# Turning the inner rows of a feed-forward block on VectorE and through DRAM instead of on TensorE

## The chip, the cores and the metric

The kernel runs on one core of a Trainium2 chip. The metric is the device time of one execution, in microseconds (us). Engines: TensorE (PE), VectorE (DVE), ScalarE (ACT), GpSimd (POOL) and SyncE (SP, which here only issues DMA transfers).

## The reference

Two transformer blocks on 256 rows of width 1024, all float32. They hold four feed-forward parts, f0 to f3, which the change touches; the mixers between them stay as they are.

```
def swiglu(h, w_gu, w_down):
    g, u = jnp.split(h @ w_gu, 2, axis=-1)      # 1024 -> 2 x 2816
    return (jax.nn.silu(g) * u) @ w_down        # 2816 -> 1024

x = x + 0.5 * swiglu(rmsnorm(x, ffn1_norm), ffn1_wgu, ffn1_wdown)        # f0
...                                                                      # mixer
x = x + 0.5 * swiglu(rmsnorm(x, ffn2_norm), ffn2_wgu, ffn2_wdown)        # f1
x = x + gate * e
x = x + 0.5 * gt1 * rmsnorm_2(swiglu_2(h, w_gu1, w_dn1), g_post)         # f2
...                                                                      # mixer
x = x + 0.5 * gt3 * rmsnorm_2(swiglu_2(h, w_gu2, w_dn2), g_post)         # f3
mods = silu(c) @ w_ada + b_ada     # 1024 -> 9 x 1024, gives sc, sh, gt
```

## The kernel before, in words

**Products.** Each float32 operand is split into a high and a low half (`hi` rounded to fp32r, `lo` the rest), and a product is three matmuls: hi x hi, hi x lo, lo x hi. The weights come through a ring: SP loads "units" of 512 KB into `raw` (8 places; `load_unit` waits until PE has used the unit seven places back, `used`), ACT makes `w_hi` (L636, `hi_part`), DVE makes `w_lo` (L1151, `lo_part`), and PE takes 12 matmuls of 512 columns for a unit. ACT and DVE run through the same order of units; `w.to(n)` in their programs handles all units up to n + 1. A unit of the up product is two transfers of 256 KB (L522, L523), with runs of 1 KB.

**A feed-forward part.** `ffn_part(f)` stands once in each engine's program. `up` is the first unit of the up product, `dn` that of the down product. The inner width 2816 is handled in 11 blocks j (`UPB`) of 256 columns, four units each. PE accumulates gate and up columns of block j in PSUM (`acc(t, j % 2)`, t = 0, 1 the row tiles of 128); ACT takes SiLU of the gate columns into `sg` (L788); DVE multiplies into `hid` (L1383 or L1386), 128 rows by 256 columns per t, two buffers. The down product needs the inner index on the partitions, so `turn_hidden(f, j - 1)` has PE transpose `hid` in four 128x128 transposes (L2182) into a PSUM bank, during block j; ACT copies it into `hid_hi` (L802, `hidden_hi`), DVE the rest into `hid_lo` (L1407, `hidden_lo`). The turn of the last block stands at k = 2 of the down product.

**The down product** goes over 22 chunks k of 128 inner columns, one unit each. `first_down` does k = 0 and 1, the column half 1 first (`n` = 1), then half 0, whose accumulators are those of the last block. Then come `row_unit` for k = 2 to 17, and `last_rows` or `last_halves` for k = 18 to 21 (`SKEW` = 4). Before chunk k PE waits for `hid_lo_ready` of its block.

**What else runs in these stages.** In f0, f1 and f2 POOL loads 24 rows `ada` of 512 KB each (three buffers, L549), and DVE adds them up (L1422, `ada_products`, 16 during the up product as `ADA_AT` lays out, 8 during the down product), with `fold_mods` (a 32x32-block transpose of 128x1024, L1435, and a sum) after blocks 6 and 10. POOL also loads `grow`, a row of gains that the gate stage after f1 wants. The order of the work on each engine is written out by hand.

Of the kernel before, what the change touches and what calls it, by code (L numbers as in the profile page):

```python
# [17 lines left out]
F32 = mybir.dt.float32  # L18
# [110 lines left out]
def two_blocks(nc, A, consts, out):  # L129
    ctx = ExitStack()  # L130
    with ctx:
# [87 lines left out]
        sg, _, e = place("sg", [P, 2, T, HALF], F32, HB)  # L219
        hid, _, END = place("hid", [P, 2, T, HALF], F32, e)  # L220
        assert END <= nc.sbuf_usable_end, (END, nc.sbuf_usable_end)
# [63 lines left out]
        oat, _, e = place("oat", [P, T, D], F32, e)  # L285

        ps = ctx.enter_context(nc.psum_tensor("ps", [P, 8, 512], F32))

        def acc(t, s):
            return ps[:, 2 * t + s, :]  # L290

        def wide(t):
# [123 lines left out]
        MODS = {"f2": 0, "mix2": 1, "f3": 2}  # L416
        FFN = ["f0", "f1", "f2", "f3"]

        ROOTS = ["f2_1", "f2_post0", "mix2_0", "f2_post1", "mix2_1", "gla",
# [91 lines left out]
        @block.sync  # L511
        def _(sp):
            def load_unit(u):
                src, nk, n = units[u]
                if u >= RING:
                    sp.wait_ge(used, u - RING + 1)
                dst = raw[:, u % RING, 0:nk * n].rearrange("p (c n) -> p c n", c=nk)
                if len(src) == 1:
                    sp.dma_start(dst, src[0]).then_inc(landed[u % RING], 16)
                else:  # L520

                    sp.dma_start(dst[:, :, 0:n // 2], src[0]).then_inc(landed[u % RING], 16)  # L522
                    sp.dma_start(dst[:, :, n // 2:n], src[1]).then_inc(landed[u % RING], 16)  # L523

            xs = A["x"][0].rearrange("(t p) d -> p t d", p=P)
            for i in range(XQ):
                c = slice(i * XW, (i + 1) * XW)
                sp.dma_start(x[:, :, c], xs[:, :, c]).then_inc(sem(f"x_landed{i}"), 16)
                load_unit(i)
            for u in range(XQ, NU):  # L530
                load_unit(u)
            for t in range(T):
                for n in range(2):
                    c = slice(512 * n, 512 * (n + 1))
# [6 lines left out]
        def _(pool):  # L541
# [69 lines left out]
            pool.dma_start(pin[:, :, :], A["p"][0, 0].rearrange("(t p) d -> p t d", p=P)).then_inc(sem("pin_landed"), 16)  # L611
            load_ada(ADA_F + 3, ADA_F + 9)
            pool.dma_start(grow[:, :], A["ple_norm"][0].partition_broadcast(P)).then_inc(sem("grow_landed"), 16)
            load_ada(ADA_F + 9, 2 * ADA_F + 3)
            load_brow(2)
# [15 lines left out]
        def _(act):  # L631
# [139 lines left out]
            def ffn_part(f):  # L771
                up, dn = ffn[f]
                for j in range(UPB):
                    w.to(up + 4 * j + 6)
                    if j == 0 and f < 2:
                        act.wait_ge(sem("rstd_ready"), NORM[FFN[f]] + 1)
                    if j == 1 and f == 0:
                        act.wait_ge(sem("par_ready"), 1)
                        act.activation(csil[:, :], par[:, :, ROW[("c_2", 0)]], ACT.Silu).then_inc(sem("csil_ready"), 1)
                    if j >= 1:  # L780
                        hidden_hi(f, j - 1)
                    if j < UPB - 1:
# [16 lines left out]

            def hidden_hi(f, j):  # L800
                act.wait_ge(sem("hid_turned"), f * UPB + j + 1)
                act.activation(hid_hi[:, 2 * j:2 * j + 2, :].rearrange("p c n -> p (c n)"), ps[:, 4 + j % 2, :], ACT.Copy)\  # L802
                   .then_inc(sem("hid_hi_ready"), 1)

# [341 lines left out]
        def _(dve):  # L1146
# [211 lines left out]
            def ffn_part(f):  # L1358
                up, dn = ffn[f]
                for j in range(UPB):  # L1360
# [5 lines left out]
                    if f == 0 and j == 2:  # L1366
# [3 lines left out]
                        dve.tensor_copy(maskD[:, :], const[:, C_D:C_D + P]).then_inc(sem("mask_ready"), 1)  # L1370
                    if j >= 1:
                        hidden_lo(f, j - 1)
                    take_mods(FFN[f], j - 1)
                    if f < 3:
                        ada_products(ADA_F * f + ADA_AT[j], ADA_AT[j + 1] - ADA_AT[j])
                    if j < UPB - 1:
                        w.to(up + 4 * j + 8)
                    for t in range(T):
                        dve.wait_ge(sem("silu_ready"), 2 * (f * UPB + j) + t + 1)
                        if j >= 2:  # L1380
                            dve.wait_ge(sem("hid_turned"), f * UPB + j - 1)
                        if f < 2:
                            i = dve.scalar_tensor_tensor(hid[:, j % 2, t, :], acc(t, j % 2)[:, HALF:], rstd[:, t:t + 1],  # L1383
                                                         sg[:, j % 2, t, :], ALU.mult, ALU.mult)
                        else:
                            i = dve.tensor_tensor(hid[:, j % 2, t, :], sg[:, j % 2, t, :], acc(t, j % 2)[:, HALF:], ALU.mult)  # L1386
# [4 lines left out]
                hidden_lo(f, UPB - 1)  # L1391
                for n in range(4):
                    if f < 3:
                        ada_products(ADA_F * f + ADA_AT[UPB] + 2 * n, 2)
                    w.to(dn + 8 + 3 * n)
                    if n == 1:
                        take_mods(FFN[f], UPB)
# [5 lines left out]

            def hidden_lo(f, j):
                dve.wait_ge(sem("hid_hi_ready"), f * UPB + j + 1)
                dst, hf = (b[:, 2 * j:2 * j + 2, :].rearrange("p c n -> p (c n)") for b in (hid_lo, hid_hi))
                dve.tensor_tensor(dst, ps[:, 4 + j % 2, :], hf.bitcast(F32), ALU.subtract).then_inc(sem("hid_lo_ready"), 1)  # L1407

# [521 lines left out]
        def _(pe):  # L1930
# [180 lines left out]
            def ffn_part(f, late=None):  # L2111
                up, dn = ffn[f]
                for j in range(UPB):
# [5 lines left out]
                    for i in range(4):  # L2119
# [3 lines left out]
                        if f == 0 and j == 0 and i == 3:  # L2123
# [4 lines left out]
                            ins.then_inc(sem("par_turned"), 1)  # L2128
                        if j >= 1 and i == (2 if j == 1 else 1):
                            turn_hidden(f, j - 1)  # L2130
                        if i == 3:
                            sum_mods(FFN[f], j)
                for k in range(FC - SKEW):
                    if k == 2:
                        turn_hidden(f, UPB - 1)
                    if f == 1 and k == 8:

                        pe.wait_ge(sem("pin_landed"), 16)
                        pe.wait_ge(sem("hid_lo_ready"), f * UPB + UPB)
# [12 lines left out]
                    if k == 14:  # L2152
                        sum_mods(FFN[f], UPB + 1)
                pe.wait_ge(sem("hid_lo_ready"), f * UPB + UPB)
                if f == 2:
# [4 lines left out]
            def first_down(f, u):  # L2160

                for n in (1, 0):
                    if n == 0:
                        pe.wait_ge(sem("hid_ready"), f * UPB + UPB)
                    for k in range(2):
# [7 lines left out]
                        if n == 0:  # L2173
                            i.then_inc(used, 1)

            def turn_hidden(f, j):
                pe.wait_ge(sem("hid_ready"), f * UPB + j + 1)
                if j >= 2:
                    pe.wait_ge(sem("hid_lo_ready"), f * UPB + j - 1)
                for c in range(2):  # L2180
                    for t in range(T):
                        i = pe.transpose(ps[:, 4 + j % 2, c * S + t * P:c * S + (t + 1) * P], hid[:, j % 2, t, c * P:(c + 1) * P], ident)  # L2182
                i.then_inc(sem("hid_turned"), 1)

# [441 lines left out]
```

## Time and profile before

| | us |
|---|---|
| median of 3 runs | 1356.03 |
| lowest, highest | 1356.00, 1356.04 |
| span of the profiled execution | 1354.2 |
| profiled execution outside its span, against the median | 1.8 |
| PE busy | 1339.0 (99%) |
| DVE busy | 930.6 (69%) |
| ACT busy | 749.4 (55%) |
| DMA, mean over the span | 200 GB/s |

The span runs from the first to the last instruction. Matmuls overlap in the array, so a PE row's duration is longer than the distance between two starts. The DMA share is the mean busy share of 16 engines; a stretch can show a little over 1. The granted PE clock is given as a share of full speed.

### The profile page before, as it was taken

To read this page: it belongs to the slowest core of one execution; us is meant where nothing else is said; L and a number is where in the kernel's file an instruction comes from. 1 tells how busy PE (TensorE), PEld (TensorE's weight loads), DVE (VectorE), ACT (ScalarE), POOL (GpSimd) and SP (SyncE) were. 2 spreads that over 40 slices of the span, in tenths; PEclk is the share of its full clock that TensorE was granted. 3 is DMA by queue.
4 is the path that set the end of the run, shared out by engine and by line. 5 is a ranking of instruction groups with operands and counts; after the bars stand their busy time and mean duration, and the time that the engine had idled before them with its cause. 6 is when DMAs were issued, how large, how long until landed. Compare 5 with 4: busy or idle time off the path is not lost.

```text
span 1354.2 us, 17190 instructions
## 1 busy us (share of the span) xinstructions
PE 1339.0 (99%) x6599; PEld 1117.7 (83%) x6599; DVE 930.6 (69%) x1334; ACT 749.4 (55%) x1169; POOL 67.2 (5%) x132
## 2 busy tenths in 40 slices
PE   9999999999999999999999999999999999999998
PEld 6888888888888888888788888889988888788886
DVE  6677867856656777877767787678866455755553
ACT  6444448567864544446845444766457664744442
POOL 3100100000000000010000010100000000000000
PEclk9999999999999999999999999999999999999999
DMA  9888866543376678885577885665544355556662
GB/s 282 290 262 277 310 199 190 167 117 108 100 243 195 214 252 272 289 288 167 168 245 250 279 290 150 202 173 159 168 140 112 108 172 169 166 180 184 187 190 88
DMA packets 167057, 270.89 MB, mean 200 GB/s; under 512 B 14242, under 2 KB 114826, under 8 KB 166976
## 3 DMA queue, kind: packets, MB, share of 16 engines
q1 hardware_dynamic: 154240, 226.66, 53.8%
q0 software_dynamic: 12576, 43.06, 9.5%
q8 instruction: 53, 0.87, 0.3%
q14 instruction: 28, 0.23, 0.0%
q10 hardware_dynamic: 160, 0.07, 0.0%
HBM read 268.66 MB, written 1.05 MB: 199 GB/s over the span
## 4 chain that ended last, share of the span: by engine, by line
PE 94%; DVE 3%; ACT 1%; DMA 1%; issue 0%; POOL 0%; DVEq 0%; SPq 0%; ACTq 0%
PE ps L1982 25%; PE ps L1947 16%; PE ps L1949 16%; PE ps L1948 16%; PE ps L2171 2%; PE ps L1961 1%; PE ps L2182 1%; PE ps L1962 1%; PE ps L1963 1%; PE ps L2065 1%; PE ps L2067 1%; PE ps L2066 1%; PE ps L2488 1%; PE ps L1997 1%; PE ps L2086 1%; PE ps L2255 1%
## 5 line engine op out<-in xcount | busy, mean ns | idle before, releaser
L1151 DVE TENSOR_TENSOR w_lo<-raw,w_hi 128x1024 fp32r<-128x1024 f32 (+2 forms) x431 | 515.1, 1214 | 249.1 <-ACT w_hi L636 246.9
L636 ACT ACTIVATE w_hi<-raw 128x1024 fp32r<-128x1024 f32 (+2 forms) x431 | 448.5, 1054 | 330.5 <-DMA raw<-in_ffn_wgu_dram 92.8
L1947 PE MATMUL ps<-w_hi,a_hi 128*128 128x512 f32 (+1 forms) x976 | 390.5, 400 | 1.1 <-DVE w_lo L1151 0.8
L1949 PE MATMUL ps<-w_hi,a_lo 128*128 128x512 f32 (+1 forms) x976 | 379.5, 389 | 0.0
L1948 PE MATMUL ps<-w_lo,a_hi 128*128 128x512 f32 (+1 forms) x976 | 378.5, 388 | 0.0
L1949 PEld LDWEIGHTS ps<-w_hi,a_lo 128*128 128x128 f32 x976 | 183.3, 188 | 38.8
L1947 PEld LDWEIGHTS ps<-w_hi,a_hi 128*128 128x128 f32 x976 | 183.6, 188 | 36.1 <-DVE w_lo L1151 1.0
L1948 PEld LDWEIGHTS ps<-w_lo,a_hi 128*128 128x128 f32 x976 | 183.8, 188 | 34.6
L1982 PE MATMUL ps<-w_hi,hid_hi 128*128 128x512 f32 x300 | 93.5, 393 | 0.0
L1982 PE MATMUL ps<-w_lo,hid_hi 128*128 128x512 f32 x300 | 92.5, 390 | 0.0
L1982 PE MATMUL ps<-w_hi,hid_lo 128*128 128x512 f32 x300 | 92.5, 390 | 0.0
L1422 DVE SCALAR_TENSOR_TENSOR acc_m<-ada,csil,acc_m 128x1024 f32<-128x1024 f32 x63 | 80.7, 1281 | 5.9 <-DMA ada<-in_w_ada_dram 2.4
L1982 PEld LDWEIGHTS ps<-w_hi,hid_lo 128*128 128x128 f32 x300 | 56.3, 188 | 11.9
L1982 PEld LDWEIGHTS ps<-w_lo,hid_hi 128*128 128x128 f32 x300 | 56.3, 188 | 11.8
L1982 PEld LDWEIGHTS ps<-w_hi,hid_hi 128*128 128x128 f32 x300 | 55.4, 188 | 10.8
L549 POOL DMA_DIRECT2D ada<-in_w_ada_dram x72 | 38.1, 530 | 440.1 <-DVE acc_m L1422 273.4
L1961 PE MATMUL ps<-a_hi,w_hi 128*128 128x256 f32 x160 | 45.9, 287 | 0.0
L1982 PE MATMUL ps<-w_hi,a_hi 128*128 128x512 f32 x144 | 45.4, 396 | 0.5 <-DVE a_lo L1355 0.5
L1963 PE MATMUL ps<-a_lo,w_hi 128*128 128x256 f32 x160 | 45.3, 283 | 0.0
L1962 PE MATMUL ps<-a_hi,w_lo 128*128 128x256 f32 x160 | 45.3, 283 | 0.0
L1982 PE MATMUL ps<-w_lo,a_hi 128*128 128x512 f32 x144 | 44.4, 390 | 0.0
L1982 PE MATMUL ps<-w_hi,a_lo 128*128 128x512 f32 x144 | 44.4, 390 | 0.0
(433 smaller groups left out, 1640.4 us busy)
## 6 DMA issues: line engine op xcount, KB each, us to landing
raw<-in_ffn_wgu_dram SPq DMA_DIRECT2D x176, 256.0 KB, 4.2
raw<-in_w_in_dram SPq DMA_DIRECT2D x88, 512.0 KB, 3.7
raw<-in_w_gu_dram SPq DMA_DIRECT2D x176, 256.0 KB, 3.3
ada<-in_w_ada_dram POOLq DMA_DIRECT2D x72, 512.0 KB, 5.4
raw<-in_ffn_wdown_dram SPq DMA_DIRECT2D x44, 512.0 KB, 4.6
raw<-in_w_dn_dram SPq DMA_DIRECT2D x44, 512.0 KB, 4.3
raw<-in_w_in_dram SPq DMA_DIRECT2D x36, 256.0 KB, 3.1
raw<-in_w_out_dram SPq DMA_DIRECT2D x16, 512.0 KB, 4.1
```

The lines of the kernel that those rows point to most:

```text
L549: pool.dma_start(ada[:, i % 3, :], w_ada[k, :, m * D:(m + 1) * D]).then_inc(sem(f"ada_landed{i % 3}"), 16)
L636: act.activation(w_hi[:, u % RING, 0:nk * n], raw[:, u % RING, 0:nk * n], ACT.Copy).then_inc(hi_ready, 1)
L1151: dve.tensor_tensor(w_lo[:, u % RING, 0:nk * n], raw[:, u % RING, 0:nk * n], w_hi[:, u % RING, 0:nk * n].bitcast(F32), ALU.subtract).then_ ...
L1422: ins = dve.scalar_tensor_tensor(acc_m[:, m % 2, :], ada[:, i % 3, :], csil[:, k:k + 1], acc_m[:, m % 2, :], ALU.mult, ALU.add)
L1947: pe.matmul(dst(t)[:, 0:n], a[0], slot(u, w_hi, kk, n), start=kc == 0, stop=False)
L1948: pe.matmul(dst(t)[:, 0:n], a[0], slot(u, w_lo, kk, n), start=False, stop=False)
L1949: i = pe.matmul(dst(t)[:, 0:n], a[1], slot(u, w_hi, kk, n), start=False, stop=kc == KC - 1)
L1961: pe.matmul(dst, hi, a_hi[:, kc, :], start=kc == 0 and q % 2 == 0, stop=False, skip_group_check=True)
L1962: pe.matmul(dst, lo, a_hi[:, kc, :], start=False, stop=False, skip_group_check=True)
L1963: i = pe.matmul(dst, hi, a_lo[:, kc, :], start=False, stop=kc == KC - 1, skip_group_check=True)
L1982: i = pe.matmul(ps[:, bank + 2 * t + n, :], a[x_], slot(u, w_, 0, D, 512 * n, 512 * (n + 1)), start=kc == 0 and x_ == 0 and w_ is w_hi, st ...
L2171: i = pe.matmul(ps[:, 2 * t + n, :], a[x_], slot(u + k, w_, 0, D, 512 * n, 512 * (n + 1)), start=k == 0 and x_ == 0 and w_ is w_hi, stop=F ...
```

## The change

PE no longer transposes `hid`. DVE turns the rows of each block by 32x32 blocks (`turn_blocks`, two transposes of 128x256, from `hid`, now one buffer, into `turned_even` or `turned_odd`, which collect two blocks). For a group m of two blocks (6 groups for 11 blocks, the last holds one), SP writes the collected 128x1024 to DRAM in one transfer, using the output tensor's memory (`passed`), and reads it back in four transfers of 32 partitions each (`gathered`), so that the 32x32 blocks come to stand at their places. ACT and DVE make `hid_hi` and `hid_lo` from `gathered`, a group at a time, in the steps of blocks 3, 5, 7 and 9 and twice in the down product. SP does this between its weight loads: in front of unit `up + 4 n + 11 + i` (n the blocks in hand, i = 0 to 3); i = 0 waits for the turned blocks and for the previous group's `hidden_lo` and writes, i = 2 waits for the write to land and issues two reads, i = 3 two more. On POOL, `grow` is loaded six `ada` rows later and after the last read of f1.

```diff
-        hid, _, END = place("hid", [P, 2, T, HALF], F32, e)
+        hid, _, e = place("hid", [P, T, HALF], F32, e)
+        turned_even, _, END = place("turned_even", [P, 4, T, 4, 32], F32, e)
+        turned_odd, _, _ = place("turned_odd", [P, 4, T, 4, 32], F32, B0 + 4096)
+        gathered, _, _ = place("gathered", [P, 4, T, 4, 32], F32, KD0)
...
+        passed = out[0, 0:P, :].rearrange("p (q t c u) -> p q t c u", q=4, t=T, c=4)
...
+        HGROUPS = (UPB + 1) // 2
...
+            def gather_hidden(f, m, i):
+                g = HGROUPS * f + m
+                if i == 0:
+                    sp.wait_ge(sem("blocks_turned"), f * UPB + min(2 * m + 2, UPB))
+                    if g >= 1:
+                        sp.wait_ge(sem("hid_lo_ready"), g)
+                    sp.dma_start(passed, turned(m)[:, :, :, :, :]).then_inc(sem("hid_moved"), 16)
+                elif i >= 2:
+                    sp.wait_ge(sem("hid_moved"), 80 * g + 16)
+                    for q in (2 * i - 4, 2 * i - 3):
+                        sp.dma_start(gathered[32 * q:32 * q + 32, :, :, :, :].rearrange("p i t c u -> p i (t c u)"),
+                                     passed[:, q, :, :, :].rearrange("(i p) t c u -> p i (t c u)", i=4)).then_inc(sem("hid_moved"), 16)
+            gather_at = {}
+            for f in range(4):
+                for m in range(HGROUPS):
+                    for i in range(4):
+                        gather_at[ffn[f][0] + 4 * min(2 * m + 2, UPB) + RING + 3 + i] = (f, m, i)
...
             for u in range(XQ, NU):
+                if u in gather_at:
+                    gather_hidden(*gather_at[u])
                 load_unit(u)
...   # POOL
-            load_ada(ADA_F + 3, ADA_F + 9)
+            load_ada(ADA_F + 3, 2 * ADA_F)
+            pool.wait_ge(sem("hid_moved"), 80 * 2 * HGROUPS)
             pool.dma_start(grow[:, :], A["ple_norm"][0].partition_broadcast(P)).then_inc(sem("grow_landed"), 16)
...   # ACT, ffn_part and hidden_hi
-                    if j >= 1:
-                        hidden_hi(f, j - 1)
                     if j < UPB - 1:
                         w.to(up + 4 * j + 8)
+                    if j >= 3 and j % 2 == 1:
+                        hidden_hi(f, j // 2 - 1)
...
-                w.to(dn + 5)
-                hidden_hi(f, UPB - 1)
+                w.to(dn + 8)
+                hidden_hi(f, HGROUPS - 2)
+                w.to(dn + 12)
+                hidden_hi(f, HGROUPS - 1)
...
+            def hidden_hi(f, m):
+                n = 2 * min(2, UPB - 2 * m)
+                act.wait_ge(sem("hid_moved"), 80 * (HGROUPS * f + m + 1))
+                for t in range(T):
+                    i = act.activation(hid_hi[:, 4 * m:4 * m + n, t * P:(t + 1) * P].rearrange("p c (i u) -> p c i u", u=32),
+                                       gathered[:, :, t, 0:n, :].rearrange("p i c u -> p c i u"), ACT.Copy)
+                i.then_inc(sem("hid_hi_ready"), 1)
...   # DVE, ffn_part: hidden_lo(f, m) at the same places, likewise a group at a time
-                        if j >= 2:
-                            dve.wait_ge(sem("hid_turned"), f * UPB + j - 1)
+                        if f + j > 0:
+                            dve.wait_ge(sem("blocks_turned"), f * UPB + j)
...
                     i.then_inc(sem("hid_ready"), 1)
+                    turn_blocks(f, j)
...
+            def turn_blocks(f, j):
+                c = 2 * (j % 2)
+                dve.wait_ge(sem("hid_ready"), f * UPB + j + 1)
+                g = HGROUPS * f + j // 2
+                if j % 2 == 0 and g >= 2:
+                    dve.wait_ge(sem("hid_moved"), 80 * (g - 1))
+                for t in range(T):
+                    i = dve.transpose(turned(j // 2)[:, :, t, c:c + 2, :], hid[:, t, :].rearrange("p (c q u) -> p q c u", c=2, u=32))
+                i.then_inc(sem("blocks_turned"), 1)
...   # PE
-                        if j >= 1 and i == (2 if j == 1 else 1):
-                            turn_hidden(f, j - 1)
...
-                    if k == 2:
-                        turn_hidden(f, UPB - 1)
-                    pe.wait_ge(sem("hid_lo_ready"), f * UPB + k // 2 + 1)
+                    pe.wait_ge(sem("hid_lo_ready"), HGROUPS * f + k // 4 + 1)
...   # PE, first_down
-                    if n == 0:
-                        pe.wait_ge(sem("hid_ready"), f * UPB + UPB)
+                    pe.wait_ge(sem("hid_ready"), f * UPB + UPB - n)
```

## Rows read from the trace of the kernel before

**Rows 1.** page: span, busy time per engine, chain that ended last by engine

```profile
span 1354.2 us, 17190 instructions
...
PE 1339.0 (99%) x6599; PEld 1117.7 (83%) x6599; DVE 930.6 (69%) x1334; ACT 749.4 (55%) x1169; POOL 67.2 (5%) x132
...
PE 94%; DVE 3%; ACT 1%; DMA 1%; issue 0%; POOL 0%; DVEq 0%; SPq 0%; ACTq 0%
```

**Rows 2.** view by stretches: busy us (x instructions) per engine, PE clock, DMA share, GB/s

```profile
51.00:63.00 12.00, 12.00 (x58) 9.94 (x57) 8.67 (x9) 5.34 (x7) 1.06 (x2) 1.00 1.02 350
155.00:160.00 5.00, 5.00 (x24) 4.14 (x23) 2.39 (x3) 2.12 (x2) 0.00 (x0) 1.00 1.03 410
15.00:136.00 121.00, 121.00 (x561) 99.94 (x560) 90.91 (x115) 61.28 (x81) 15.59 (x29) 1.00 0.87 278
415.00:538.00 123.00, 122.88 (x570) 101.38 (x569) 89.58 (x120) 65.56 (x92) 6.34 (x12) 1.00 0.73 231
660.00:785.00 125.00, 124.95 (x573) 103.06 (x574) 90.55 (x111) 64.56 (x94) 8.47 (x16) 1.00 0.75 241
1170.00:1292.00 122.00, 122.00 (x558) 100.90 (x558) 70.24 (x80) 63.03 (x84) 0.00 (x0) 1.00 0.62 190
```

**Rows 3.** timeline of PE: start us, us, engine, line, operation; around one `turn_hidden`

```profile
669.59 0.39 PE L1947 MATMUL ps<-w_hi,a_hi 128*128 128x512 f32 x1
...
677.52 0.40 PE L1949 MATMUL ps<-w_hi,a_lo 128*128 128x512 f32 x1
...
697.55 0.39 PE L1949 MATMUL ps<-w_hi,a_lo 128*128 128x512 f32 x1
...
698.13 0.48 PE L1947 MATMUL ps<-w_hi,a_hi 128*128 128x512 f32 x1
...
699.37 0.39 PE L1949 MATMUL ps<-w_hi,a_lo 128*128 128x512 f32 x1
```

**Rows 4.** groups of instructions by line: count, busy us, mean ns, idle before

```profile
L1407 DVE TENSOR_TENSOR hid_lo<-ps,hid_hi 128x512 fp32r<-128x512 f32 x44 | 30.2, 686 | 10.9 <-ACT hid_hi L802 10.9
...
L2182 PE MATMUL ps<-const,hid 128*128 128x128 f32 x176 | 26.4, 272 | 0.0
...
L802 ACT ACTIVATE hid_hi<-ps 128x512 fp32r<-128x512 f32 x44 | 25.9, 589 | 30.1 <-PE ps L2182 30.1
...
L1435 DVE STREAM_TRANSPOSE ps<-acc_m 128x1024 f32<-128x1024 f32 x6 | 7.5, 1250 | 0.0
```

**Rows 5.** timeline of SP's queue, first halves of weight loads in f0

```profile
56.77 0.37 SPq L522 DMA_DIRECT2D raw<-in_ffn_wgu_dram  x1
...
62.21 0.37 SPq L522 DMA_DIRECT2D raw<-in_ffn_wgu_dram  x1
...
65.40 0.37 SPq L522 DMA_DIRECT2D raw<-in_ffn_wgu_dram  x1
...
76.77 0.37 SPq L522 DMA_DIRECT2D raw<-in_ffn_wgu_dram  x1
```

**Rows 6.** timeline in f0: DVE, ACT, DVE at 59 to 65 us; DVE, PE at 137

```profile
59.53 0.87 DVE L1383 SCALAR_TENSOR_TENSOR hid<-ps,rstd,sg 128x256 f32<-128x256 f32 x2
...
63.54 1.06 ACT L636 ACTIVATE w_hi<-raw 128x1024 fp32r<-128x1024 f32 x1 [3.51 <-DMA raw<-in_ffn_wgu_dram]
...
64.64 1.23 DVE L1151 TENSOR_TENSOR w_lo<-raw,w_hi 128x1024 fp32r<-128x1024 f32 x1 [3.10 <-ACT w_hi L636]
...
137.06 0.88 DVE L1383 SCALAR_TENSOR_TENSOR hid<-ps,rstd,sg 128x256 f32<-128x256 f32 x2 [0.61 <-ACT sg L788]
...
139.07 0.39 PE L2171 MATMUL ps<-w_hi,hid_hi 128*128 128x512 f32 x1
```

**Rows 7.** DMA issues: count, KB each, median us from issue to landing

```profile
raw<-in_ffn_wgu_dram SPq DMA_DIRECT2D x176, 256.0 KB, 4.2
...
ada<-in_w_ada_dram POOLq DMA_DIRECT2D x72, 512.0 KB, 5.4
...
out_dram<-x SPq DMA_DIRECT2D x4, 256.0 KB, 2.0
```

More of the change, by code:

```diff
@@ L290, in acc, with turned @@
             return ps[:, 2 * t + s, :]
+        def turned(m):
+            return turned_odd if m % 2 else turned_even
         def wide(t):
@@ L611, in _ @@
             pool.dma_start(pin[:, :, :], A["p"][0, 0].rearrange("(t p) d -> p t d", p=P)).then_inc(sem("pin_landed"), 16)
-            load_ada(ADA_F + 3, ADA_F + 9)
+            load_ada(ADA_F + 3, 2 * ADA_F)
+            pool.wait_ge(sem("hid_moved"), 80 * 2 * HGROUPS)
             pool.dma_start(grow[:, :], A["ple_norm"][0].partition_broadcast(P)).then_inc(sem("grow_landed"), 16)
-            load_ada(ADA_F + 9, 2 * ADA_F + 3)
+            load_ada(2 * ADA_F, 2 * ADA_F + 3)
             load_brow(2)
@@ L798, in ffn_part @@
                 w.to(dn + FC + (1 if f == 2 else 2))
[L800 to L803, printed above, removed]
+            def hidden_hi(f, m):
[5 more added lines that the diff above has]
+                i.then_inc(sem("hid_hi_ready"), 1)
             def weigh2(i):
@@ L1370, in ffn_part @@
                         dve.tensor_copy(maskD[:, :], const[:, C_D:C_D + P]).then_inc(sem("mask_ready"), 1)
-                    if j >= 1:
-                        hidden_lo(f, j - 1)
                     take_mods(FFN[f], j - 1)
@@ L1377, in ffn_part @@
                         w.to(up + 4 * j + 8)
+                    if j >= 3 and j % 2 == 1:
+                        hidden_lo(f, j // 2 - 1)
                     for t in range(T):
                         dve.wait_ge(sem("silu_ready"), 2 * (f * UPB + j) + t + 1)
-                        if j >= 2:
-                            dve.wait_ge(sem("hid_turned"), f * UPB + j - 1)
+                        if f + j > 0:
+                            dve.wait_ge(sem("blocks_turned"), f * UPB + j)
                         if f < 2:
-                            i = dve.scalar_tensor_tensor(hid[:, j % 2, t, :], acc(t, j % 2)[:, HALF:], rstd[:, t:t + 1],
+                            i = dve.scalar_tensor_tensor(hid[:, t, :], acc(t, j % 2)[:, HALF:], rstd[:, t:t + 1],
                                                          sg[:, j % 2, t, :], ALU.mult, ALU.mult)
                         else:
-                            i = dve.tensor_tensor(hid[:, j % 2, t, :], sg[:, j % 2, t, :], acc(t, j % 2)[:, HALF:], ALU.mult)
+                            i = dve.tensor_tensor(hid[:, t, :], sg[:, j % 2, t, :], acc(t, j % 2)[:, HALF:], ALU.mult)
                     i.then_inc(sem("hid_ready"), 1)
+                    turn_blocks(f, j)
                     if f < 3 and j in (6, 10):
@@ L1390, in ffn_part @@
                 w.to(dn + 5)
-                hidden_lo(f, UPB - 1)
                 for n in range(4):
@@ L1395, in ffn_part @@
                     w.to(dn + 8 + 3 * n)
+                    if n == 0:
+                        hidden_lo(f, HGROUPS - 2)
+                    if n == 1:
+                        w.to(dn + 12)
+                        hidden_lo(f, HGROUPS - 1)
                     if n == 1:
@@ L1402, in ffn_part, with hidden_lo @@
                 w.to(dn + FC + (1 if f == 2 else 2))
[L1404 to L1407, printed above, removed]
+            def turn_blocks(f, j):
[7 more added lines that the diff above has]
+                i.then_inc(sem("blocks_turned"), 1)
+            def hidden_lo(f, m):
+                n = 2 * min(2, UPB - 2 * m)
+                dve.wait_ge(sem("hid_hi_ready"), HGROUPS * f + m + 1)
+                for t in range(T):
+                    dst, hf = (b[:, 4 * m:4 * m + n, t * P:(t + 1) * P].rearrange("p c (i u) -> p c i u", u=32) for b in (hid_lo, hid_hi))
+                    i = dve.tensor_tensor(dst, gathered[:, :, t, 0:n, :].rearrange("p i c u -> p c i u"), hf.bitcast(F32), ALU.subtract)
+                i.then_inc(sem("hid_lo_ready"), 1)
             def ada_products(i0, n):
@@ L2133, in ffn_part @@
                 for k in range(FC - SKEW):
-                    if k == 2:
-                        turn_hidden(f, UPB - 1)
                     if f == 1 and k == 8:
                         pe.wait_ge(sem("pin_landed"), 16)
-                        pe.wait_ge(sem("hid_lo_ready"), f * UPB + UPB)
                         for c in range(2):
@@ L2153, in ffn_part @@
                         sum_mods(FFN[f], UPB + 1)
-                pe.wait_ge(sem("hid_lo_ready"), f * UPB + UPB)
+                pe.wait_ge(sem("hid_lo_ready"), HGROUPS * f + HGROUPS)
                 if f == 2:
@@ L2174, in first_down @@
                             i.then_inc(used, 1)
[L2176 to L2183, printed above, removed]
             def sum_mods(key, j):
```

## Prediction

> **What bounds the kernel now.** I read the page's busy shares first, then the chain that ended last: TensorE (PE) is busy 99% of the span and carries 94% of the chain; VectorE (DVE) stands at 69%, ScalarE (ACT) at 55% [rows 1]. So time is won only by taking instructions out of PE's stream, and lost only where another engine or a transfer makes PE wait. Next, the stretches of the four feed-forward blocks (f0 to f3). The reader is to see three things there: PE is practically never idle (122.88 busy of 123 us at worst), its granted clock is 1.00 (the 2.4 GHz level), and the DMA share differs much: 0.87 in the first, 0.73 and 0.75 in the next two, 0.62 in the last, where no `ada` rows are loaded [rows 2]. Last, the timeline of PE around one `turn_hidden`, and the timelines of the weight loads and of ACT and DVE behind them, for the slack.
>
> **What is removed.** 176 PE transposes of 128x128 in 44 groups of four. A transpose lasts 272 ns by its row [rows 4], but these durations overlap, so its price on the path is read from start times. From the matmul ahead of the group (697.55) to the sixth matmul behind it (699.37) it is 1.82 us [rows 3]; six steps of the undisturbed spacing (669.59 to 677.52 is 35 of them, so 0.227 us [rows 3]) are 1.36. The group costs 0.46 us: the four transposes themselves, and a late first matmul behind them (698.13, 0.58 us after the last one ahead). The queue of weight loads says the same from another side: a load is released by each unit that PE ends, two undisturbed steps, 56.77 to 62.21, are 5.44, so 2.72 us a unit, and 62.21 to 65.40, where a group lies between, is 3.19 [rows 5]: 0.47. I take 0.465: 44 x 0.465 = **20.5 us**.
>
> The Trainium skill (TensorE: Matmul & The Clock Gate, Part 4: PE-mode transpose) gives about 275 ns for a transpose within a kernel. The trace agrees on the duration (272), and somebody who priced the path by it would take off 176 x 0.272 = 47.9 us and forecast 1308; the spacing of the starts speaks against that reading.
>
> **What is added on DVE.** Two 32x32-block transposes of 128x256 per inner block, 88 in all. No row has this shape; the nearest is the transpose of 128x1024 at 1250 ns [rows 4]. Bounds: a quarter of it, 0.31 us, and the whole of it, 1.25 us, should the four-dimensional patterns run badly. I take 0.33, because the row is elementwise work of a steady rate. Each of the two steps also waits for its own engine's last instruction (the row buffer `hid` is single now), some 0.1 us each as an estimate. So +0.9 us per block. `hidden_lo` and `hidden_hi` handle as many elements as before, 512 per partition for a block (686 and 589 ns [rows 4]), only from SBUF and two blocks at a time: I take no change. DVE's work per block: 90.9 us of 121 in f0 [rows 2], times the block's length of 11.35 us (four units of 2.72 and one group) = 8.5; after, 9.4 of a block of 10.88: 87%. At the upper bound, 8.5 + 2 x 1.25 + 0.3 = 11.3, over 10.88 by 0.4.
>
> **What is added on the DMA.** Per two blocks one write of 512 KB (4 KB a partition) and four reads of 128 KB (1 KB runs): 24 groups, the last of each f as large as the others, 25 MB. Near rates: f0 moves 278 GB/s at a share of 0.87, which is 320 at a full share; the best stretch moves 410 at 1.03 [rows 2], 398. So 1.05 MB takes 3.3 or 2.6 us of all engines. A pair of blocks lasts 2 x 10.88 = 21.8 us after, 22.7 before. With 3.3: f0 needs 0.87 x 22.7 + 3.3 = 23.0 (106%), f1 0.73: 19.9, f2 0.75: 20.3, f3 0.62: 17.4. By bytes f0 needs (278 x 22.7 + 1050)/21.8 = 338 GB/s, below the 350 of 51 to 63 us and the 410. So f0 comes to the edge, the others do not: nothing to (23.0 - 21.8) x 5 = 6 us. I take 1.5, since the rows with the highest rates show that the share of a crowded stretch overstates the need.
>
> The Trainium skill (DMA: Bandwidth & Descriptors, Where 436 GB/s comes from) puts the HBM limit of a core at about 358 GB/s. The stretch at 410 goes beyond it, so the trace does not bear it out as a hard limit; by it f0 would still fit, at 94%.
>
> **What is moved, and who stands behind it.** SP now issues the write and the reads in the stream of weight loads, and waits three times: for the turned blocks, for the previous `hidden_lo`, and, two units later, for its own write to land. The write is issued three units (8.2 us) after PE ended its second block; DVE's `hid` of a block is over 3.6 us after PE's end (PE's end of block 3 releases the load at 56.77, and `hid` runs from 59.53 for 0.87 [rows 5, 6]), so the first wait is met. The second is late once per f: group 5 wants `hidden_lo` of group 4, which stands behind the weights of dn+9; SP stops there for about two units (5 us). Behind SP wait the weight loads, with this slack: in crowded f0 the load issued at 56.77 is taken by ACT at 63.54, its low half starts at 64.64, and PE reaches it at 76.77, when the load seven places further is released [rows 5, 6]: 76.77 - 65.87 = 10.9 us. A stop of 5 us is covered. If that cover is gone, what is late next is the low half of a unit, and PE stands.
>
> ACT and DVE now wait for the reads ahead of SiLU and `hid` of every odd block from the third on. Normally the reads are released about two units before PE ends that block, so they land near its end; in f0, where a load took 6.8 us, SiLU comes some 2 to 4 us late. The accumulators of that block are wanted again a block later (10.9 us): no stall. At the head of the down product, the second half now waits for the last `hid` directly: it starts at 139.07, `hid` ends by 137.94 [rows 6], 1.1 us of margin, unchanged because block 10 has no gather ahead of it. In the tail, group 4 is first wanted at k = 16 and group 5 at k = 18; the last reads of group 5 go out at about k = 7 and land two units later, so nine units (24 us) are left: hidden. On POOL the `grow` load moves behind six `ada` loads and the last read of f1; it is wanted only by the gate stage, after the down product.
>
> **Sum.** Profiled execution: span 1354.2, 1.8 below the 1356.03 median. 1354.2 - 20.5 + 1.5 = 1335.2 in the span; 1356.03 - 20.5 + 1.5 = **1337.0**.
>
> **Rivals.**
> - *f0 becomes bound by transfers* (22%). For it: share 0.87 and landing times up to 6.8 us [rows 2, 5, 6]; against: 350 and 410 GB/s elsewhere. 4 to 9 us are lost: 1339.5 to 1344.5.
> - *DVE's transposes are dear* (8%). At 1.25 us each, 0.4 us x 11 blocks in f0, and about half of it in each of f1 and f2: some 8 us back, 1343.5. Even the upper bound does not eat the gain.
> - *The round trip closes a loop, and the kernel gets slower* (9%). Write of group m -> landing W -> reads with the loads between them 2.7 us (six issues of 0.37 us and more, and the gaps between them [rows 5]) -> landing R -> `hidden_hi` 1.2 -> `hidden_lo` 1.4 (twice the durations of [rows 4]) -> `hid` 0.9 -> turn 0.8, semaphores 0.5 -> write of m+1. That is W + R + 7.5 against 21.8 us for two blocks, four such turns in each f. It bites from W + R = 14.3 and eats the whole gain at 20.5/16 = 1.3 us more, 15.6. Landing rows: 4.2 for a pair of weight halves, 5.4 for `ada`, 2.0 for the 256 KB store [rows 7], 6.8 at worst: W + R is 6 to 14. At 17 it would be 1356 - 20.5 + 16 x 2.7 = 1379.
> - *The change gives nothing* (4%): PE's freed time turns into waits at other places, 1354 to 1358. Against it: the stretches show no idle PE, and the low halves are ready 10.9 us ahead.
> - *A gain by the full duration of the transposes* (1%), 1308.
>
> The Trainium skill (DMA: Bandwidth & Descriptors, Anatomy of one DMA) says that a completion can take surprisingly long when the write goes to HBM, and puts the fixed part at about 2.0 us. No row here shows a store in a crowded stretch; by its fit W would be 3.2 us and the loop stays open.
>
> **How the numbers follow.** All hidden or nearly (1335 to 1338.5): 52%. The cases above 22, 8, 9, 4, 1; the last 4% are losses between 1345 and 1353. 1334 to 1346 holds the first three, 82%. Faster by over 0.2% (2.7 us, about what a measurement can tell) holds 52 + 22 + 8 + 1 + 4 = 87%, within 4%, slower 9%.
>
> **What would show it.** Right: no PE row for the transposes of `hid`; spacing of weight loads 2.72 us without the 3.19 steps; PE still at 99%; a DVE transpose row near 330 ns x88; the f1 to f3 stretches 5 us shorter each. f0's DMA share near 1.0, f0 perhaps shortened less. Wrong: idle of PE ahead of the up product's matmuls put to `w_lo` or to `hid`; SP's waits for `out` rows to land of several us; a transpose row above 0.9 us; ACT's wait ahead of `hid_hi` growing beyond a unit in f1 to f3.

## The result

| | us |
|---|---|
| changed kernel, median of 4 runs | 1378.04 |
| lowest, highest | 1375.18, 1380.36 |
| kernel before beside it, median of 4 | 1356.01 |
| ratio | 1.0163, 95% interval 1.0147 to 1.018 |
| forecast | 1337.0, range 1334 to 1346, faster |

The change makes the kernel 1.6% slower. One execution of the kernel before, taken beside the last set of experiments, ran at 1915.1 us with a granted clock of 0.654 and is left out of every comparison. The profiled execution of the changed kernel took 1376.63 with a span of 1374.8. The page of the changed kernel, with its busy times and its chain, answers to [rows 1]:

```profile
span 1374.8 us, 17076 instructions
...
PE 1325.1 (96%) x6423; PEld 1103.4 (80%) x6423; DVE 961.1 (70%) x1426; ACT 747.4 (54%) x1173; POOL 67.1 (5%) x132
...
PEclk9999989999999999999999998999999999999999
DMA  9999946543365699994489996555553345578982
...
PE 80%; DMA 8%; DVE 5%; issue 3%; ACT 2%; SPq 1%; DVEq 0%; POOL 0%; ACTq 0%
```

The time can be split by two numbers of each page. Before: 1339.0 of PE work and 15.2 of PE idle in 1354.2 us [rows 1]. After: 1325.1 of work and 49.7 of idle. Work fell by 13.9, not by 20.5, and idle grew by 34.5. PE also carries 80% of the chain now and no longer 94%. Slice 6 of 40 in the clock row (172 to 206 us) and slice 25 (825 to 859) stand at 8; two of the stands of PE lie there.

The view of PE's own waits says where the idle time is (us in total, times, longest):

```profile
PE ps L2237 <- issue: 26.9, 3, 9.9
PE ps L2220 <- DVE hid L1419: 2.8, 2, 2.2
...
PE ps L2241 <- DVE rs L1491: 1.9, 1, 1.9
```

L2237 is the first matmul of the gate sum, `sum_mods` after chunk k = 14 of the down product, in f0, f1 and f2. It waits for `gate_lo` on DVE. Three stands (stretches in which PE is idle because a wait isn't met) take 26.9 us. In the timeline of PE, f0:

```profile
177.41 0.61 PE L2037 MATMUL ps<-w_hi,hid_lo 128*128 128x512 f32 x2
187.88 0.77 PE L2237 MATMUL ps<-m_hi,onesr 128*128 128x512 f32 x1 [9.85 <-issue]
188.45 0.63 PE L2238 MATMUL ps<-m_lo,onesr 128*128 128x512 f32 x1
...
189.73 1.05 PE L2037 MATMUL ps<-w_hi,hid_hi 128*128 128x512 f32 x2
190.58 1.05 PE L2037 MATMUL ps<-w_lo,hid_hi 128*128 128x512 f32 x2
...
192.09 0.62 PE L2037 MATMUL ps<-w_hi,hid_hi 128*128 128x512 f32 x2
```

Two matmuls took 0.62 us together before the stand, and 1.05 behind it. From 187.88 to 192.09 PE starts 10 matmuls, 2.27 us of work at 0.227; it took 4.21. So a stand of 10 costs 12. The stretch view shows why: the granted clock is 0.72 over the 15 us that hold the stand, and 0.52, the 1.2 GHz level, in the 4 us behind it. The last row below, f0's up product, answers to [rows 2].

```profile
160.00:175.00 15.00, 14.25 (x63) 11.47 (x63) 8.82 (x14) 6.39 (x8) 0.53 (x1) 1.00 1.04 335
175.00:190.00 15.00, 5.13 (x17) 3.93 (x18) 11.55 (x11) 6.74 (x7) 0.00 (x0) 0.72 0.35 126
188.00:192.00 4.00, 4.00 (x10) 3.14 (x11) 3.97 (x4) 0.98 (x2) 0.00 (x0) 0.52 0.00 0
15.00:133.00 118.00, 116.09 (x519) 95.36 (x518) 93.72 (x130) 60.04 (x79) 15.06 (x28) 1.00 1.04 314
```

The Trainium skill (TensorE: Matmul & The Clock Gate, Why this matters for your kernels) warns that idle gaps between matmul bursts bring the clock down. The trace agrees: 0.72 in the stretch of the stand.

**Who kept DVE.** The timeline of DVE in f0, from the wait to `gate_lo` (L1496):

```profile
161.83 1.23 DVE L1187 TENSOR_TENSOR w_lo<-raw,w_hi 128x1024 fp32r<-128x1024 f32 x1 [0.22 <-ACT w_hi L667]
168.45 1.23 DVE L1187 TENSOR_TENSOR w_lo<-raw,w_hi 128x1024 fp32r<-128x1024 f32 x1 [5.39 <-ACT w_hi L667]
169.60 0.76 DVE L1461 TENSOR_TENSOR hid_lo<-gathered,hid_hi 128x256 fp32r<-128x256 f32 x2
...
171.07 2.66 DVE L1477 SCALAR_TENSOR_TENSOR acc_m<-ada,csil,acc_m 128x1024 f32<-128x1024 f32 x2
173.66 2.35 DVE L1187 TENSOR_TENSOR w_lo<-raw,w_hi 128x1024 fp32r<-128x1024 f32 x2
...
179.61 1.28 DVE L1477 SCALAR_TENSOR_TENSOR acc_m<-ada,csil,acc_m 128x1024 f32<-128x1024 f32 x1 [2.41 <-DMA ada<-in_w_ada_dram]
181.00 1.21 DVE L1484 TENSOR_TENSOR acc_m<-acc_m,brow 1x1024 f32<-1x1024 f32 x1
...
184.28 2.36 DVE L1187 TENSOR_TENSOR w_lo<-raw,w_hi 128x1024 fp32r<-128x1024 f32 x2 [0.93 <-ACT w_hi L667]
186.56 1.22 DVE L1496 TENSOR_TENSOR m_lo<-acc_m,m_hi 128x1024 fp32r<-128x1024 f32 x1
```

It stood 5.39 us for the high half of dn+13, which the changed order wants ahead of the last group's `hidden_lo`; then the last `ada` rows came late, 2.41 us more (POOL could issue their load only at 172.65, when DVE had freed the buffer); then everything in front of `gate_lo` followed. The weights of dn+13 were late because SP had stopped, and because they took long to land. SP's queue in f0, ACT at these weights, and SP's waits over the span:

```profile
144.17 0.43 SPq L527 DMA_DIRECT2D raw<-in_ffn_wdown_dram  x1
153.46 0.36 SPq L540 DMA_DIRECT2D out_dram<-turned_odd  x1
153.87 1.44 SPq L527 DMA_DIRECT2D raw<-in_ffn_wdown_dram  x2
157.07 1.05 SPq L544 DMA_DIRECT2D gathered<-out_dram  x2
158.16 0.48 SPq L527 DMA_DIRECT2D raw<-in_ffn_wdown_dram  x1
```

```profile
167.36 1.06 ACT L667 ACTIVATE w_hi<-raw 128x1024 fp32r<-128x1024 f32 x1 [5.56 <-DMA raw<-in_ffn_wdown_dram]
```

```profile
SPq L539 <- DVE hid_lo L1461: 34.4, 4, 9.3
...
SPq L544 <- DMA out_dram<-turned_odd: 15.3, 10, 3.6
SPq L544 <- DMA out_dram<-turned_even: 9.6, 4, 4.4
...
SPq L540 <- DVE turned_even L1453: 1.7, 2, 1.5
```

L539 is the wait for the previous group's `hidden_lo`, 34.4 us in four stops, each ahead of the last group's write. In f0 no weight load left SP between 144.17 (dn+10) and 153.87 (dn+11). As an estimate, dn+13 would have been issued three units of 2.72 us after dn+10, at 152.3; it was issued at 158.16, some 6 us late. ACT had it at 167.36, 9.2 us after its issue, where the median landing of these loads was 4.6 us in the kernel before. So in f0 both the stop and the slower landing made `gate_lo` late.

In the kernel before, the same place had almost no margin. DVE's `gate_lo` and PE's gate sum in its f0:

```profile
175.48 1.22 DVE L1441 TENSOR_TENSOR m_lo<-acc_m,m_hi 128x1024 fp32r<-128x1024 f32 x1
```

```profile
177.90 0.40 PE L2197 MATMUL ps<-m_hi,onesr 128*128 128x512 f32 x1
```

`gate_lo` ended at 176.70 and PE came at 177.90: 1.2 us. In f1 there was no margin at all:

```profile
601.69 1.22 DVE L1441 TENSOR_TENSOR m_lo<-acc_m,m_hi 128x1024 fp32r<-128x1024 f32 x1
```

```profile
603.00 0.47 PE L2197 MATMUL ps<-m_hi,onesr 128*128 128x512 f32 x1
```

`gate_lo` ended at 602.91, and PE, which by its spacing of 0.227 would have come at 602.76, came at 603.00. The view of PE's waits doesn't list so short a stand. In f2 `gate_lo` ended at 822.75 and PE came at 825.01: 2.3 us.

Groups and landings of the changed kernel, which answer to [rows 4] and [rows 7]:

```profile
L1461 DVE TENSOR_TENSOR hid_lo<-gathered,hid_hi 128x512 fp32r<-128x512 f32 (+1 forms) x48 | 28.9, 643 | 4.2 <-ACT hid_hi L837 3.6
...
L837 ACT ACTIVATE hid_hi<-gathered 128x512 fp32r<-128x512 f32 (+1 forms) x48 | 25.9, 588 | 6.4 <-DMA gathered<-out_dram 5.9
...
L1453 DVE STREAM_TRANSPOSE turned_even<-hid 128x256 f32<-128x256 f32 x48 | 18.5, 424 | 0.8
```

```profile
raw<-in_ffn_wgu_dram SPq DMA_DIRECT2D x176, 256.0 KB, 6.0
...
ada<-in_w_ada_dram POOLq DMA_DIRECT2D x72, 512.0 KB, 7.1
raw<-in_ffn_wdown_dram SPq DMA_DIRECT2D x44, 512.0 KB, 7.9
...
gathered<-out_dram SPq DMA_DIRECT2D x96, 128.0 KB, 6.1
...
out_dram<-turned_even SPq DMA_DIRECT2D x12, 512.0 KB, 5.7
```

First matmuls of the four down products: 136.4, 560.7, 783.5 and 1287.6 us in the trace before, 133.3, 570.3, 798.6 and 1308.8 after. So f0's up product gained 3.1 us, the stretches from one of these points to the next, which hold the gate sums, lost 12.7, 5.5 and 6.1, and f3's down product, without a gate sum, gained 0.6.

### The profile page after: what moved, and what is told of

The parts are those of the page before. It is cut to its first block, busy times and chain, and to the rows that moved or that the text cites. A ratio compares the mean times of both kernels' runs of the same rounds, so it can differ in the third digit from the quotient of the medians.

```text
span 1374.8 us, 17076 instructions
## 1 busy us (share of the span) xinstructions
PE 1325.1 (96%) x6423; PEld 1103.4 (80%) x6423; DVE 961.1 (70%) x1426; ACT 747.4 (54%) x1173; POOL 67.1 (5%) x132
## 4 chain that ended last, share of the span: by engine, by line
PE 80%; DMA 8%; DVE 5%; issue 3%; ACT 2%; SPq 1%; DVEq 0%; POOL 0%; ACTq 0%
PE ps L2037 20%; PE ps L2002 14%; PE ps L2004 14%; PE ps L2003 14%; DMA gathered<-out_dram 3%; PE ps L2016 1%; PE ps L2017 1%; PE ps L2018 1%; DVE w_lo L1187 1%; DMA raw<-in_ffn_wgu_dram 1%; DMA out_dram<-turned_odd 1%; PE ps L2120 1%; PE ps L2528 1%; PE ps L2122 1%; PE ps L2121 1%
## 5 line engine op out<-in xcount | busy, mean ns | idle before, releaser
L2002 PE MATMUL ps<-w_hi,a_hi 128*128 128x512 f32 (+1 forms) x976 | 386.5, 396 | 1.3 <-DVE w_lo L1187 1.0
```

The costliest lines, as they stand in the source:

```text
L2002: pe.matmul(dst(t)[:, 0:n], a[0], slot(u, w_hi, kk, n), start=kc == 0, stop=False)
```

## The experiments

PE work and idle are the busy time and the rest of the span on each page. "Easing" names the reorderings of e4 and e6 below.

| kernel | median | ratio to before, 95% | PE work | PE idle |
|---|---|---|---|---|
| before | 1356.0 | 1 | 1339.0 | 15.2 |
| changed | 1378.0 | 1.0163 (1.0147 to 1.018) | 1325.1 | 49.7 |
| d1: no transfers | 1338.0 | 0.9864 (0.985 to 0.9879) | 1318.4 | 18.8 |
| d2: before + traffic | 1388.7 | 1.0236 (1.0218 to 1.0253) | 1350.7 | 40.0 |
| d3: the same, SP doesn't wait | 1385.7 | 1.021 (1.0173 to 1.0247) | 1348.0 | 39.7 |
| e1: gate sum at 16 | 1358.0 | 1.0011 (0.999 to 1.0032) | 1322.5 | 24.5 |
| e2: last group late | 1356.2 | 0.9994 (0.9978 to 1.001) | 1325.9 | 30.1 |
| e3: both | 1344.9 | 0.992 (0.9892 to 0.9949) | 1321.2 | 22.6 |
| e4: and `gate_lo` first | 1342.2 | 0.9892 (0.987 to 0.9913) | 1320.6 | 21.5 |
| e5: last block on PE | 1348.1 | 0.9941 (0.9923 to 0.996) | 1324.0 | 23.8 |
| e6: e4 with eased head | 1342.7 | 0.9894 (0.9875 to 0.9912) | 1318.4 | 17.4 |
| c1: before, eased | 1355.0 | 0.9997 (0.9988 to 1.0007) | 1339.0 | 14.3 |
| d4: d3, eased | 1363.2 | 1.0058 (1.0043 to 1.0073) | 1340.3 | 24.3 |
| d5: d1, eased | 1336.9 | 0.9868 (0.9851 to 0.9884) | 1317.7 | 16.4 |

Each ratio is to runs of the kernel before taken beside that kernel (medians 1355.3 to 1356.0). Work and idle are of one execution each, and compare only roughly: the page of e1 is of its fastest execution of ten (1348.8), those of e6 and d5 are of their fastest of four, those of d1, d2, d3, d4 and e4 of their slowest of four. The kernels with transfers spread by up to 13 us between executions (e1: 1348.8 to 1361.9), where the kernel before spreads by 5.4 at most (1354.5 to 1359.8 in nine).

**d1, no transfers.**

```diff
-                if u in gather_at:
-                    gather_hidden(*gather_at[u])
-                act.wait_ge(sem("hid_moved"), 80 * (HGROUPS * f + m + 1))
+                act.wait_ge(sem("blocks_turned"), f * UPB + min(2 * m + 2, UPB))
-                                       gathered[:, :, t, 0:n, :]   # in hidden_hi, hidden_lo alike
+                                       turned(m)[:, :, t, 0:n, :]
```

> The changed kernel without any transfer: hidden_hi and hidden_lo read the turned buffers directly (so the 32x32 blocks are not exchanged between partitions and the products are of wrongly placed rows); SP issues no write and no read, everything else stays. Theory A (PE stands at k = 14 of the down products of f0, f1 and f2, because gate_lo comes late on DVE behind the last group's round trip): without the round trip the group costs DVE only its own work, the three stands of 9 to 10 us go, and the 20.5 us of the transposes are paid out: 1336 to 1342. Rival B (DVE's own added work and the later w.to(dn + 12) are enough to make gate_lo late): the stands stay in part, 1350 to 1365.

1338.0. PE work fell by 20.6 us, the estimate for the transposes. The round trip costs 40 us. Gate stands of 4.0 us are left of 26.9, so DVE's new order alone is not free: rival B, that this order delays `gate_lo` by itself, holds for that small part.

**d2, traffic alone, in the kernel before.**

```diff
+                    sp.dma_start(passed, x[:, 0, :]...).then_inc(sem("hid_moved"), 16)        # i = 0, after the last group's reads
+                    sp.wait_ge(sem("hid_moved"), 80 * g + 16)                                 # i = 2
+                        sp.dma_start(gathered[32 * q:32 * q + 32, ...], passed[:, q, ...])    # i = 2, 3
...
+                pe.wait_ge(sem("hid_moved"), 80 * HGROUPS * (f + 1))                          # ahead of chunk 18
```

> The kernel before, with its PE transposes, and only the traffic added: at the same places SP writes 512 KB (from x, row tile 0) to the output's memory, waits for it to land and reads it back in four transfers into memory that nobody uses; PE waits for the last group's reads before the last four chunks. SP doesn't wait for hidden_lo here. Theory A: the traffic by itself makes landings later, by 1 to 3 us in f0, with 1.2 us of margin ahead of the gate sum: 1358 to 1366. Rival C (volume of the DMA engines is the bound): the full loss shows without any change on PE or DVE, 1378 + 20 = 1390 or more.

1388.7, about what the rival on the traffic (C) named (1390 or more), on a kernel whose instructions on PE and DVE are untouched. My theory had put the traffic at 10 us at most. PE's waits, though, are not for weights:

```profile
PE ps L2222 <- issue: 17.0, 3, 7.0
PE ps L2207 <- DVE hid L1407: 6.3, 4, 3.5
```

L2222 is the gate sum, L2207 the transposes of `hid`. SP waits here too: 23.7 us in four stops for the previous group's reads, ahead of the last group's write, and 19.4 us between the writes and the reads.

**e1, gate sum at 16.**

```diff
-                    if k == 14:
+                    if k == 16:
                         sum_mods(FFN[f], UPB + 1)
```

> The changed kernel with one number changed: PE takes the gate sum (sum_mods with the ones matrix) after chunk k = 16 instead of 14, two units or 5.4 us later. Theory A: each of the three stands shrinks by 5.4 us, and the clock is lost for a shorter time or not: 1378 - 16 = 1362, down to 1357. Rival C (PE waits for data of the transfers): the stands only move to another instruction, 1376 to 1380.

1358.0: 20 us back for one number, within the range. It is above the 16 of the three shorter stands alone, and the clock is kept as well: 0.994 to 0.999 as the mean of each of the ten executions, against 0.987 to 0.989 in the changed kernel.

**e2, last group late.**

```diff
-gather_at[ffn[f][0] + 4 * min(2 * m + 2, UPB) + RING + 3 + i] = (f, m, i)
+gather_at[ffn[f][0] + 4 * min(2 * m + 2, UPB) + RING + (6 if m == HGROUPS - 1 else 3) + i] = (f, m, i)
...   # ACT: hidden_hi(f, HGROUPS - 1) behind m_hi; DVE:
-                        w.to(dn + 12)
-                        hidden_lo(f, HGROUPS - 1)
...
                     gate_lo(f)
+                hidden_lo(f, HGROUPS - 1)
```

> The changed kernel with the last group (block 10) put off: its write and reads stand three units later in SP's queue, hidden_hi of it behind m_hi on ACT, hidden_lo behind gate_lo on DVE, and DVE's w.to(dn + 12) ahead of it is dropped. Theory A: SP no longer stops for hidden_lo of group 4, the weights dn+11 to dn+13 come in time, gate_lo is done near k = 14; what is left is the loss at the end of f0's up product (about 4 us): 1338 to 1344. Rival C (volume): at most a few us better than 1378.

1356.2: 22 us back, but 12 short of the forecast. SP's wait for `hidden_lo` fell from 34.4 to 2.3 us, and gate stands of 10.1 us stay. The run moves three things at once: SP's transfers of the last group, its `hidden_lo` on DVE, and the `w.to(dn + 12)` ahead of it. So it doesn't show how much of the 22 us was SP's stop. That stands are left shows that the stop was not all of it.

**d3, the bytes without any wait for them.**

```diff
-                    sp.wait_ge(sem("hid_moved"), 80 * g + 16)
-                                     passed[:, q, :, :, :]...
+                                     A["attn_proj"][0][0:P, 256 * q:256 * (q + 1)].rearrange("(i p) n -> p i n", i=4)
...   # the last group three units later
```

> As d2 (the kernel before plus traffic), but nobody in SP's queue waits for it: the four reads take their 1 KB runs from a weight matrix instead of the memory just written, and the last group's transfers stand three units later, so the previous group's have long landed. Same bytes, same run lengths. Theory A (what hurts is that SP stops, for the write's landing and ahead of the last group, and holds the weight loads back): most of the 33 us of d2 goes, 1358 to 1365. Rival C (the bytes themselves, in queues that are full in the first three feed-forward parts): 1378 to 1390, with the landing times of the weights as in d2 (8 us for the down weights of f0 and f1).

1385.7: again rival C's number. SP's queue no longer waits for any transfer of `hid` (43.1 us in d2, none here), and that is worth 3 us, with intervals that overlap; the bytes do the rest. The down weights of f0 and f1 land after 8.4 us (median), against 4.6 in the kernel before. Again the waits are at the gate sum (12.7 us) and for `hid` (9.5).

**e3 and e4.** e3 is e1 and e2 together. e4 adds:

```diff
+                    if n == 3 and f < 3:
+                        gate_lo(f)
                     w.to(dn + 8 + 3 * n)
...
-                if f < 3:
-                    gate_lo(f)
```

> The changed kernel with both edits of before: the gate sum at k = 16, and the last group put off. Either alone gave 1356 to 1358 with stands of about 3 to 10 us left. Theory A: together the stands at the gate sum go altogether; what is left over the 1338 of the kernel without transfers is the wait at the head of the down product: 1340 to 1345. Rival C (volume): PE's waits move to the weights, 1350 or more.

> e3_both, and on DVE gate_lo stands ahead of the three weight units dn+16 to dn+18 instead of behind them, 3.6 us of work and a wait for ACT earlier. Theory A: no stand at the gate sum is left in any execution, so the time and its spread both fall to 1339 to 1342. If e3 has none left, the same as e3.

1344.9 and 1342.2, both at the upper end of their ranges; the spread fell from 8.2 us in e3 to 3.5 in e4. With e4 the same traffic runs as in the changed kernel, and PE's list of waits no longer has the gate sum. In f0 PE is now busy through the stretch where it stood:

```profile
15.00:133.00 118.00, 116.31 (x520) 95.47 (x519) 93.37 (x130) 59.41 (x79) 15.06 (x28) 1.00 1.02 313
160.00:175.00 15.00, 15.00 (x68) 12.43 (x67) 11.72 (x14) 3.81 (x5) 0.53 (x1) 1.00 1.04 323
175.00:190.00 15.00, 15.00 (x67) 12.39 (x67) 13.17 (x13) 10.37 (x12) 0.54 (x1) 1.00 0.75 249
```

**e5, the last block on PE.** Its own transfers fall away, and PE takes back four transposes per feed-forward part.

```diff
+                    if k == 2:
+                        for c in range(2):
+                            for t in range(T):
+                                i = pe.transpose(ps[:, 5, c * S + t * P:c * S + (t + 1) * P], hid[:, t, c * P:(c + 1) * P], ident)
+                        i.then_inc(sem("blocks_turned"), 1)
...   # SP: for m in range(HGROUPS - 1)
```

> As e4, but the last block (10) of each feed-forward part is again transposed by PE at k = 2 of the down product and doesn't go through DRAM: 20 groups of transfers instead of 24 (the saved ones fall in the fullest stretch), 4 groups of PE transposes back (4 x 0.465 = 1.9 us). Theory A: no stands, 1340 to 1344. Rival C (volume): this one is the fastest of all with transfers, by 5 us or more over e4.

1348.1, outside the forecast and slower than e4, with a sixth less traffic; rival C had forecast the opposite. Of PE's work on the pages, 3.4 us more, the 16 transposes are 1.9 (16 x 0.116); the rest is the lower clock and a longer wait for `hid` at the head of the down products (7.3 us in three places). I can't say from these runs why that wait grew; it varies between executions.

**c1, d4, d5 and e6: the same easing on four kernels.** To e4's edits come two:

```diff
-                    w.to(up + 4 * j + 6)                              # ACT and DVE
+                    w.to(up + 4 * j + (6 if j < UPB - 1 else 4))
-                    if k == 4:                                        # PE
+                    if k == 5:
                         sum_mods(FFN[f], UPB)
```

> The kernel before, with the four reorderings that ease the changed one: gate sum at k = 16, gate_lo ahead of the weights dn+16 to dn+18, the sum after block 10 at k = 5 instead of 4, and ACT and DVE take the weights dn+2 and dn+3 behind the last block's SiLU and product instead of ahead. Theory A: the kernel before hardly stands at any of these places (1.2 us of margin was enough), so it gains nothing: 1354 to 1357. A rival: the gain of e4 over the kernel before comes from the reorderings and not from the transposes: 1345 or less.

> d3 (the kernel before plus the traffic alone, 1386) with the same four reorderings. Theory A' (the added bytes cost time through the few waits that have a microsecond of margin, above all the gate sum and the heads of hid, and not because the queues can't carry them): most of the 30 us goes, 1356 to 1364. Rival C (the DMA engines are full, so each added byte costs): it stays at 1375 to 1386 and PE waits for weights.

> d1 (no transfers, blocks not exchanged between partitions, 1338) with the same four reorderings and the last group's hidden_lo behind gate_lo. This is what the PE and DVE part gives alone: d1 still had 4 us of stands at the gate sum, so 1333 to 1335.5; 1335.5 is the median before less 20.5.

> e4 (1342) with the two further reorderings, the sum at k = 5 and the two weights behind the last block's SiLU and product, against the 4 us that PE waited for hid at the head of the down products and the 1.4 us for the folded sums. Theory A': 1335 to 1339. If the round trip's lateness only moves on, the same as e4.

c1 takes the time of the kernel before: the easing gives nothing where nothing is late. d4 (1363.2) settles the dispute over the bytes: of the 30 us that they cost in d3, 22 go by moving four waits, with every byte still there. What d4 has left stands mostly at PE's transposes of `hid` (8.9 us in eight places on its page), which the changed kernel doesn't have. d5 is what PE and DVE give alone, 1336.9, above its bracket by 1.4. e6 is no better than e4 by its median (1342.7 against 1342.2); its profiled execution, 1337.6, lay within the forecast, the other three did not. Between e6 and d5 stand 5.8 us by the medians and 3.5 by the ratios, whose intervals overlap: that is the price of the round trip once nothing tight stands behind it, and it is known only as some 4 to 6 us.

## Why the prediction was wrong

**Right:** the transposes' price. 20.5 us from the spacing of starts; d1 shows 20.6 less PE work. DVE's added work did little harm by itself (d1: 1338.0, with 4.0 us of gate stands), though a transpose took 0.424 us and not 0.33, and 961.1 us of DVE work is 30.5 more than before. `hidden_hi` and `hidden_lo` cost the same. The end of block 10's product at the head of the down product had 1.1 us of margin; PE waited there 3.0 us in three places.

**The step that failed** is the one on the queues: "SP stops there for about two units (5 us). ... A stop of 5 us is covered", with the tail "hidden". The cover was computed to the weight that PE multiplies, 10.9 us, and to the group's own readers, 24 us. But ACT and DVE take everything in one order. Behind the late weight and the group's `hidden_lo` on DVE stood `ada_products` and `gate_lo`, and PE wanted `gate_lo` at k = 14 with 1.2 us to spare in f0, none in f1 and 2.3 in f2. The prediction names what is late next as "the low half of a unit". It was the gate sum: 26.9 us of stands, and about 2 us of slow clock behind each (PE's work is 6.7 us above that of d1). The stop was also longer than said, 34.4 us in four. But the stop alone doesn't explain the stands: the weights behind it landed late as well.

**A second term was mis-sized:** the traffic. I took 1.5 us for the whole kernel, all of it in f0, bound 6, and in the kernel before the same bytes cost 30 us (d3). I let the highest rows (350 and 410 GB/s) outvote the share of 0.87. f0's up product ran at a share of 1.04 and 314 GB/s, under the 338 that it wanted; the row of the share was the better guide. I also priced crowding as throughput only. It came as latency: weight halves in f0 and f1 land after 6.0 us instead of 4.2 [rows 7], and latency is paid where the margin is smallest, in f1 and f2 as well, whose shares I had called free. In the changed kernel the two causes can't be added up neatly: moving the sum (e1) or the last group (e2) took back about 20 us each of the same 40.

**The rivals.** The slower one had 9% and the right sign, with another place: a loop of write, reads, `hidden_hi`, `hid` and turn. It exists. In f0 the chain of the changed kernel runs through it (columns: start, us):

```profile
110.77 6.47 DMA out_dram<-turned_odd
119.06 9.53 DMA gathered<-out_dram
131.09 0.80 DVE hid L1419 x2
131.91 0.78 DVE turned_even L1453 x2
132.71 3.78 DMA out_dram<-turned_even
```

W + R is 16.0 there, over the 14.3 at which it was to bite. f0's up product gained 3.1 us of the 4.7 that its ten groups were worth (10 x 0.465), so loop and traffic together cost it 1.6 (2.1 against d1, whose down product begins at 131.2). The rival's own sum for W + R = 17, 1379, is nearly the measured time by luck: it put 43 us on sixteen turns of the loop, and the loss stands at the gate sums, where one number takes half of it away. The fit that gave W as 3.2 us was too low: the writes took 5.7 us from `turned_even` and 4.7 from `turned_odd` (medians). "f0 becomes bound by transfers" was right in its share and wrong in its price: f0's up product lost about 2 us and not 4 to 9.

**What is settled, and what isn't.** Shown: the transposes are worth 20.6 us of PE's work (18.8 us of time in d5, by the medians); the round trip costs 40 us as the change places it, and some 4 to 6 with the last group put off and four waits moved; most of that loss stands at one sum on PE (26.9 us, and the slow clock behind it). Not settled: in the changed kernel, the split between SP's stop, the bytes and DVE's order, and the cause of e5's longer wait.

## What to carry to other kernels

Before putting a transfer or a wait into an engine's hand-written order, list all that this engine does behind it and read for each the margin to its reader; the smallest margin sets the price, not that of the data moved. A kernel at 99% of PE can hold waits with a microsecond or nothing to spare that the list of its waits doesn't show: here `gate_lo`. Traffic that fits beside a share of 0.7 to 0.9 isn't free for that: here it lengthened the median landings of all loads of the feed-forward parts, in f2 and f3 from 3.3 to 4.1 us for the up weights and from 4.3 to 5.8 for the down weights. With such waits moved, the change pays: e4 is 1.1% faster than the kernel before (interval 0.9 to 1.3%), and the easing alone gives nothing.

## What I had not expected of the hardware

- A 128x256 block transpose on DVE, from SBUF to SBUF with the strided patterns, took 424 ns; a quarter of the 1250 ns that one of 128x1024 into PSUM took would be 312.
- 25 MB more, in a kernel that moves 271, raised the median landing of 512 KB down weights from 4.6 to 7.9 us in f0 and f1.
- A stand of PE of 9.85 us cost about 2 more at the lower clock level behind it. With the added traffic the time of this program on one core spread by up to 13 us from execution to execution (e1).
